# Routed expert rows: weighted at evacuation and summed by an accumulating scatter, in place of slots combined at the end

## The reference

```python
def moe(x, p):
    scores = sigmoid(x @ p['w_router'])                        # 1032 x 64
    _, e_idx = top_k(scores + p['router_bias'], 6)
    w = take_along_axis(scores, e_idx, axis=1)
    w = w / sum(w, axis=-1, keepdims=True) * ROUTED_SCALE
    ...
    routed = segment_sum(y_rows * row_w[:, None], row_tok)     # y_rows: swiglu of each expert on its rows
    shared = swiglu(x, p['w_sh_gate'], p['w_sh_up'], p['w_sh_down'])
    return routed + shared
x = layer_norm(DN_ALPHA * x + moe(x, p), p['ln2_g'], p['ln2_b'])
```

## Time and profile before

| what | us |
|---|---|
| median of three runs | 2399.06 (2397.37 to 2402.83) |
| the profiled execution, its own time | 2404.58 |
| its span, first to last instruction | 2402.6 |
| PE busy over the span | 2310.7 (96%) |
| DVE, ACT, POOL busy over the span | 871.5, 595.5, 341.9 |

### The profile page before, as it was taken

The page is one execution under the profiler, slowest core; times in us unless marked ns, Lnnn a source line. Parts: engine busy times, 40 slices in busy tenths (PEclk is TensorE's granted clock), DMA queues, the critical chain, the costliest instruction groups (busy, mean ns, idle before and its releaser), DMA issues.

```text
span 2402.6 us, 28164 instructions
## 1 busy us (share of the span) xinstructions
PE 2310.7 (96%) x9838; PEld 1349.4 (56%) x9838; DVE 871.5 (36%) x1733; ACT 595.5 (25%) x1288; POOL 341.9 (14%) x763
## 2 busy tenths in 40 slices
PE   8998999999999999999999999899999999999976
PEld 6455656667666666666664556445455454454422
DVE  0217888643366661001003558311111111111139
ACT  2126666554234430000001220011111111111111
POOL 0003444202000000000000000132232222222300
PEclk9998999999999999999999999999999999999978
DMA  6211000436411103111103130399999999998856
GB/s 210 99 64 34 2 2 2 163 118 246 122 31 35 31 22 111 40 40 35 40 9 111 70 123 18 104 342 353 341 350 344 346 344 347 345 345 333 322 226 267
DMA packets 127114, 389.57 MB, mean 162 GB/s; under 512 B 20660, under 2 KB 77964, under 8 KB 98336
## 3 DMA queue, kind: packets, MB, share of 16 engines
q1 hardware_dynamic: 105360, 304.02, 34.4%
q0 software_dynamic: 21664, 84.31, 9.6%
HBM read 362.02 MB, written 50.04 MB: 172 GB/s over the span
## 4 chain that ended last, share of the span: by engine, by line
PE 89%; DVE 6%; issue 2%; DMA 2%; ACT 1%; SPq 0%; ACTq 0%; DVEq 0%
PE PS L1081 26%; PE PS L1303 19%; PE PS L1314 9%; PE PS L669 8%; PE PS L782 5%; PE PS L1216 4%; PE PS L815 3%; PE PS L852 3%; PE PS L1200 2%; PE PS L952 2%; PE PS L1255 1%; PE PS L717 1%; PE PS L1352 1%; DVE arena L2264 1%; PE PS L1137 1%
## 5 line engine op out<-in xcount | busy, mean ns | idle before, releaser
L1081 PE MATMUL PS<-arena 128*128 128x344 f32 x2112 | 614.6, 453 | 3.1 <-ACT arena L1634 3.1
L1081 PEld LDWEIGHTS PS<-arena 128*128 128x128 f32 x2112 | 401.8, 190 | 214.0 <-issue 5.2
L1303 PE MATMUL PS<-arena 128*128 128x512 f32 x1056 | 464.1, 592 | 0.0
L1363 ACT ACTIVATE arena<-PS 128x512 f32<-128x512 f32 (+13 forms) x561 | 265.9, 502 | 663.0 <-PE PS L669 422.6
L669 PEld LDWEIGHTS PS<-arena 128*128 128x128 f32 (+3 forms) x1960 | 239.4, 160 | 190.8 <-issue 129.8
L669 PE MATMUL PS<-arena 128*128 128x128 f32 (+3 forms) x1960 | 292.4, 281 | 33.0 <-DVE arena L1867 8.1
L1303 PEld LDWEIGHTS PS<-arena 128*128 128x128 f32 x1056 | 195.9, 190 | 221.0 <-issue 221.0
L1314 PE MATMUL PS<-arena 128*128 128x512 f32 x528 | 242.9, 592 | 0.0
L2233 DVE TENSOR_TENSOR arena<-PS,arena 128x256 f32<-128x256 f32 x66 | 28.0, 425 | 437.7 <-ACT arena L1685 437.7
L1314 PEld LDWEIGHTS PS<-arena 128*128 128x128 f32 x528 | 95.5, 191 | 94.7 <-issue 94.7
L2298 POOL TENSOR_SCALAR arena<-arena 128x384 f32<-128x384 f32 (+3 forms) x192 | 103.2, 559 | 141.3 <-DVE arena L1844 95.8
(11 more groups left out here) (310 smaller groups left out, 2039.9 us busy)
## 6 DMA issues: line engine op xcount, KB each, us to landing
arena<-in_w_exp_gate SPq DMA_DIRECT2D x66, 1024.0 KB, 6.7
arena<-in_w_exp_up SPq DMA_DIRECT2D x66, 1024.0 KB, 8.8
arena<-in_w_exp_down SPq DMA_DIRECT2D x66, 1024.0 KB, 8.7
arena<-expert_rows SPq DMA_DIRECT2D x8, 3072.0 KB, 13.2
arena<-in_w_in SPq DMA_DIRECT2D x34, 512.0 KB, 3.8
...
```

What stands on the lines that cost most here:

```text
L1081: ins = mm(PS[:, bank + c, 0:CH], w[:, k, :], rhs[:, k, c * CH:(c + 1) * CH], start=k == 0, stop=k == kts - 1)
L1303: ins = mm(PS[:, 2 + s, :].rearrange("p (h n) -> p h n", h=2), xgT[:, s, k, :], wex[:, :, s, k, :], start=k == 0, stop=k == KT - 1)
L1363: return fn(out, in_, ACT.Copy)
```

## The change

Each token now has one row in DRAM, `acc_rows` (1032 rows of 4 KB in the memory of `expert_rows`). SP writes `x1tok` there (residual and shared expert) before the loop, and the six routed rows of a token are added to it by the scatters, whose DMA has an addition as compute operation. Because a token can be in several blocks, two scatters must not overlap: POOL waits for the landing of scatter 0 (`yd0`) before scatter 1, and for that of scatter 1 (`yd1`) before the scatter 0 of the next turn.

The weight of a routed row is multiplied in as its output is copied from PSUM: ACT's copy has a scale, DVE's copy becomes a product with a scalar per partition. The 128 weights of a block come by a small indirect gather of 4-byte elements (`weights_in`) from a table that SP writes to DRAM (`wtab`).

The loop is 32 fixed turns (64 blocks). Spare blocks follow one at a time (`spare`, all four engines, SP alike with `spare_in`), in three ranges (`SPARE`) with a branch around each. `nblk` now holds the number of blocks and the counts for which SP waits.

The tail reads the 4 MB of `acc_rows` back into `x1tok` in five transfers. For each tile DVE takes the statistics, ACT the root, DVE the reciprocal and the negative mean times it, ACT scales and shifts the whole tile, DVE multiplies by `ln2_g`, POOL adds `ln2_b`, and SP writes it out from `x1tok`. PE has no part in it.

A few semaphores are renamed and used twice (`s_load`), which changes no wait. The loop bodies of 32 turns and the branch ladder, the same on each engine, are shown for POOL alone:

```diff
+SPARE = ((NE // 2, NE // 2 + 2), (NE // 2 + 2, NE // 2 + 8), (NE // 2 + 8, NBLK // 2))
...
-        ygs = [at(o_, TOPK, D) for o_ in (4000, 30784, 36928, 45120)]
-        fin = at(10144, 2, D)
-        dg = at(21472, 2, 4, P)
+        ACC0 = 16
+        y_rows = y_dram.rearrange("b p d -> (b p) d")[0:ACC0 + NTOK, :]
+        acc_rows = y_rows[ACC0:, :]
+        wtab = y_dram.rearrange("b p d -> (b p d) ()")[0:NTOK * 8, :]
...
+        widx = rowb[:, 0, 0:2]
+        wrow = at(29700, 2)
...
+        Y_IN = {m: (s_load[k], 48 if k == 3 else 32) for k, m in enumerate((0, 1, 2, 4, 6))}
...
+            sp.wait_ge(sem("M_done"), NT)
+            sp.dma_start(wtab[0:SEQ * 8, :].rearrange("(t p k) o -> p t (k o)", p=P, k=8), wfin[:, 0:NT - 1, :]).then_inc(sem("wt_out"), 16)
...
-            turns = sp.value_load(nblk[0:1, 0:1], min_val=33, max_val=NBLK // 2)
-            with sp.Fori(1, NBLK // 2) as i:
-                with sp.If(i < turns):
...
+                sp.wait_ge(sem("acc_done"), t + 1)
+                sp.dma_start(acc_rows[t * P:t * P + n, :], x1tok[0:n, t, :]).then_inc(sem("x2_out"), 16)
+            blocks = sp.value_load(nblk[0:1, 0:1], min_val=NE, max_val=NBLK)
+            landed = [sp.value_load(nblk[0:1, 1 + s:2 + s], min_val=8 * NE, max_val=8 * NBLK) for s in range(2)]
...
+            for s in range(2):
+                sp.wait_ge(sem(f"yd{s}"), landed[s])
+            sp.wait_ge(sem("x2_out"), 16 * NT)
+            sp.dma_start(x1tok[0:BD, NT - 1, :], acc_rows[SEQ:NTOK, :]).then_inc(Y_IN[0][0], 16)
+            for (m, (s, _)), hi in zip(list(Y_IN.items())[1:], list(Y_IN)[2:] + [NT]):
+                sp.dma_start(x1tok[:, m - 1:hi - 1, :], acc_rows[(m - 1) * P:(hi - 1) * P, :].rearrange("(t p) d -> p t d", p=P)).then_inc(s, 16)
             for m, t in enumerate(TAIL):
                 n = rows_of(t)
...
                 sp.wait_ge(sem("fin_done"), m + 1)
                 dst = o["y_p"][t * P:(t + 1) * P, :] if n == P else o["y_s"]
-                sp.dma_start(dst, fin[0:n, m % 2, :]).then_inc(sem(f"y_out{m % 2}"), 16)
...
+                sp.dma_start(dst, x1tok[0:n, t, :]).then_inc(sem("y_out"), 16)
+            sp.wait_ge(sem("y_out"), 16 * NT)
...
-            with pe.Fori(0, NBLK // 2) as i:
-                with pe.If(i < turns):
...
-            for m, t in enumerate(TAIL):
-                n = rows_of(t)
-                pe.wait_ge(sem(f"y_in{m % 4}"), 16 * (m // 4 + 1))
...
+            with pe.Fori(0, NE // 2) as i:
...
+            def spare(i, s):
+                for hf in range(2):
+                    pe.wait_ge(sem(f"xgT_ev{hf}"), 2 * i + 2 + s)
+                pe.wait_ge(sem(f"wex{s}"), 32 * i + 32)
+                pe.wait_ge(sem(f"gu_free{s}"), i + 1)
+                gate_up(s, 0, KT).then_inc(sem(f"gu_mm{s}"), 1)
+                turn_hidden(i, s)
+                pe.wait_ge(sem("hT_ev"), 2 * i + s + 1)
+                pe.wait_ge(sem(f"wexd{s}"), 16 * i + 16)
+                pe.wait_ge(sem("y_ev"), 2 * i + s + 1)
+                pe.wait_ge(sem("y_ev2"), 2 * i + s + 1)
+                down(s, 0)
+                down(s, 1).then_inc(sem("y_mm"), 1)
+                turn_rows(i + 1, s, False)
...
+            def act_down(i, s, first=False):
+                act.wait_ge(sem("y_mm"), 2 * i + s + 3)
+                if not first:
+                    act.wait_ge(sem(f"yd{s}"), 16 * i)
+                act.wait_ge(sem(f"wg{s}"), 16 * i + 16)
+                fn(ysb[:, s, 512:1024], PS[:, 5 + 2 * s, :], ACT.Copy, scale=wrow[:, s:s + 1]).then_inc(sem("y_ev"), 1)
...
-            def weights_diag(m):
...
+                s, y = st[0:n, m % 2, :], x1tok[0:n, t, :]
                 act.wait_ge(sem("var_done"), NT + m + 1)
-                fn(st[0:n, m % 2, 14:15], st[0:n, m % 2, 13:14], ACT.Sqrt).then_inc(sem("std_done"), 1)
-                if m + 2 < NT:
-                    weights_diag(m + 2)
+                E.do(fn(s[:, 14:15], s[:, 13:14], ACT.Sqrt), sem("std_done"))
+                act.wait_ge(sem("mean_done"), m + 1)
+                E.do(fn(y, y, ACT.Identity, bias=s[:, 0:1], scale=s[:, 15:16]), sem("normed"))
...
-            E.step(ts(wk[0:1, 3:4], cs[0:1, NE - 1:NE], 0.5, None, ALU.mult))
-            E.step(ts(ridx[0:1, 1:NE + 0], const("exp", 1)[:, 0:NE - 1], wk[0:1, 3:4], None, ALU.is_lt))
...
-            E.step(V.tensor_copy(nblk[0:1, 0:1], wk[0:1, 4:5]), sem("table_step"))
+            E.step(ts(wk[0:1, 3:4], cs[0:1, NE - 1:NE], float(NE), None, ALU.add))
+            E.step(ts(wk[0:1, 4:5], wk[0:1, 3:4], 1.0, None, ALU.add))
+            E.step(V.tensor_copy(nblk[0:1, 0:1], wk[0:1, 3:4]))
+            E.step(V.tensor_copy(nblk[0:1, 3:4], wk[0:1, 4:5]))
+            E.step(ts(nblk[0:1, 1:2], nblk[0:1, 3:4], 1, None, ALU.logical_shift_right))
+            E.step(ts(nblk[0:1, 2:3], nblk[0:1, 0:1], 1, None, ALU.logical_shift_right))
+            E.step(ts(nblk[0:1, 1:3], nblk[0:1, 1:3], 4, None, ALU.logical_shift_left), sem("table_step"))
...
+            def dve_down(i, s, first=False):
+                dve.wait_ge(sem("y_mm"), 2 * i + s + 3)
+                if not first:
+                    dve.wait_ge(sem(f"yd{s}"), 16 * i)
+                dve.wait_ge(sem(f"wg{s}"), 16 * i + 16)
+                ts(ysb[:, s, 0:512], PS[:, 4 + 2 * s, :], wrow[:, s:s + 1], None, ALU.mult).then_inc(sem("y_ev2"), 1)
...
-            def normed_out(m):
...
-                E.step(stt(y, y, s[:, 12:13], lnw[0:n, 2, :], ALU.subtract, ALU.mult))
...
-                E.do(stt(fin[0:n, m % 2, :], y, s[:, 15:16], lnw[0:n, 3, :], ALU.mult, ALU.add), sem("fin_done"))
+            with dve.Fori(1, NE // 2) as i:
...
+            def scaled_out(m):
+                n = rows_of(TAIL[m])
+                y = x1tok[0:n, TAIL[m], :]
+                dve.wait_ge(sem("normed"), m + 1)
+                E.do(tt(y, y, lnw[0:n, 2, :], ALU.mult), sem("scaled"))
             for m, t in enumerate(TAIL):
                 n = rows_of(t)
-                acc = x1tok[0:n, t, :]
                 s = st[0:n, m % 2, :]
-                dve.wait_ge(sem(f"y_in{m % 4}"), 16 * (m // 4 + 1))
-                for k in range(VK):
-                    E.step(stt(acc, ygs[m % 4][0:n, k, :], wfin[0:n, t, k:k + 1], acc, ALU.mult, ALU.add), sem("yg_used") if k == VK - 1 else None)
-                dve.wait_ge(sem("comb_mm"), m + 1)
-                acc2 = acc.rearrange("p (a b) -> p a b", a=2)
-                E.step(tt(acc2, acc2, PS[0:n, 4 + 2 * (m % 2):6 + 2 * (m % 2), :], ALU.add), sem("acc2_done"))
-                stats(acc, s)
+                if m in Y_IN:
+                    dve.wait_ge(*Y_IN[m])
+                stats(x1tok[0:n, t, :], s)
                 if m:
-                    normed_out(m - 1)
+                    scaled_out(m - 1)
                 dve.wait_ge(sem("std_done"), NT + m + 1)
                 E.step(V.reciprocal(s[:, 15:16], s[:, 14:15]))
-            normed_out(NT - 1)
+                E.do(stt(s[:, 0:1], s[:, 12:13], -1.0, s[:, 15:16], ALU.mult, ALU.mult), sem("mean_done"))
+            scaled_out(NT - 1)
...
+            def weights_in(s):
+                G.indirect_dma_start(out=wrow[:, s:s + 1], out_offset=None, in_=wtab,
+                                     in_offset=bass.IndirectOffsetOnAxis(ap=widx[:, s:s + 1], axis=0),
+                                     bounds_check=NTOK * 8 - 1, oob_is_err=False).then_inc(sem(f"wg{s}"), 16)
+            def rows_out(i, s, first=False):
                 pool.wait_ge(sem("y_ev"), i * 2 + s + 3)
                 pool.wait_ge(sem("y_ev2"), i * 2 + s + 3)
+                if s:
+                    pool.wait_ge(sem("yd0"), 16 * i + 16)
+                elif not first:
+                    pool.wait_ge(sem("yd1"), 16 * i)
                 G.tensor_tensor(pause[:, 0:1], izero[:, 0:1], izero[:, 0:1], ALU.add)
-                G.tensor_tensor(dsts[:, s:s + 1], slotall[:, bass.ds(i * 2 + s, 1)], izero[:, 0:1], ALU.add).then_inc(sem(f"ix{s}"), 1)
-                pool.wait_ge(sem(f"ix{s}"), n)
+                G.tensor_tensor(dsts[:, s:s + 1], tokall[:, bass.ds(i * 2 + s, 1)], izero[:, 1:2], ALU.add).then_inc(sem(f"ix{s}"), 1)
+                G.tensor_tensor(widx[:, s:s + 1], slotall[:, bass.ds(i * 2 + s + 2, 1)], izero[:, 0:1], ALU.add).then_inc(sem(f"ix{s}"), 1)
+                pool.wait_ge(sem(f"ix{s}"), i * 3 + 5)
                 G.tensor_tensor(pause[:, 1:2], izero[:, 0:1], izero[:, 0:1], ALU.add)
-                G.indirect_dma_start(out=yrows, out_offset=bass.IndirectOffsetOnAxis(ap=dsts[:, s:s + 1], axis=0),
+                G.indirect_dma_start(out=y_rows, out_offset=bass.IndirectOffsetOnAxis(ap=dsts[:, s:s + 1], axis=0),
                                      in_=ysb[:, s, :], in_offset=None,
-                                     bounds_check=NTOK * 8 - 1, oob_is_err=False).then_inc(sem(f"yd{s}"), 16)
+                                     bounds_check=ACC0 + NTOK - 1, oob_is_err=False, compute_op=ALU.add).then_inc(sem(f"yd{s}"), 16)
```

(36 more changed lines are left out.)

235 lines of the change are left out of this document (119 added, 116 removed).

## The result

| | before | after |
|---|---|---|
| median, us | 2400.34 (2397.37 to 2402.83, 4 runs) | 2447.53 (2443.44 to 2454.28, 4 runs) |
| ratio, 95% interval | | 1.0199 (1.0174 to 1.0225) |
| span of the profiled execution, us | 2402.6 | 2452.5 |
| granted clock over the span | 0.980 | 0.966 |

The account below looks back on a forecast made before the run. PE was taken to bound the loop's turns and DVE to pace the tail. The terms, -8.6 - 62.9 + 1 + 28 = -42.5 us from 2399.06, gave 2356.6, stated as 2358; 8 in 10 range 2328 to 2420.

Parts of the forecast that it names:

- Part 1: Expert loop: 64 blocks in 32 turns and the 65th alone in 13.5 us instead of 22.15; gain 8.6 us.
- Part 2: From last expert matmul to the end: 44.6 us instead of 107.46, DVE tiles of 3.4 us; gain 62.9 us.
- Rival C: Tail: engines don't overlap, DVE and ACT wait for each other; 5 us a tile, 2371 us; no chance of its own.
- Part 3: Ahead of the loop: two more small DVE steps, a memset, SP's writes of tables and rows; together 1 us of loss.
- Part 4: Loop: waits for adding scatters make a 24.2 us chain to the row gather, over 22.83; 0.9 us a turn, 28 us.
- the spread: Loop: landings range from 5.2 to 9.7 us and only late ones count; 0.2 us more a turn.
- D: Loop: extra landing time of an adding scatter over a plain one; taken as 1.5 us, bounds 0 and 5.1.
- A: Loop: adding scatter lands like a plain one, the 22.2 us chain fits into 22.83; 2337 us, chance 0.21.
- B: Loop: POOL's pair of scatter waits becomes the period; slower than before, over 2400, up to 2493 us; chance 0.16.

Follow-up runs that it names:

- e4_tail_ts: Changed kernel with the tail's one-column product as a tensor_scalar reading one tensor instead of a scalar_tensor_tensor reading two; 2436.37 us, ratio 1.0158 to the kernel before.
- e1_plain: Changed kernel with the addition taken out of the scatter's DMA, all waits and other transfers kept; 2364.71 us, ratio 0.9854 to the kernel before.
- e2_noweights: Changed kernel without the gathers of weights in the loop, all weights 1; 2425.59 us, ratio 1.0103 to the kernel before.
- e3_gathers_first: Changed kernel with the row gathers issued between scatter 0 and scatter 1, one turn further ahead; 2351.07 us, ratio 0.9795 to the kernel before.
- e8_first_plain: e3_gathers_first with scatters that only store and don't add; 2352.15 us, ratio 0.9791 to the kernel before.
- e9_first_delay: e3_gathers_first with seven more small POOL steps ahead of each scatter; 2352.79 us, ratio 0.9820 to the kernel before.

## Why the prediction was wrong

**Part 1, the turns: right.** 65 blocks were run (65 scatters in the list above), the lone one in 13.0 us; 13.5 were forecast.

**Part 2, the tail: 44.6 forecast, 64.4 measured.** The order of the steps was as described. Mis-sized was the tile: of the "two small steps (0.17 each)" one took 2.33 us with its wait for POOL, which makes a tile 1.9 us longer, 15 us in all. L2272 of the earlier trace rows was rightly read, but before there was no POOL addition beside such a step. e4_tail_ts shows this for the step. The rest is smaller: the first 7.4 us took 9.0, since the last scatter landed in 4.69 us rather than 3.2, and the end after the last DVE product took 7.9 instead of 5.1: POOL's addition of 2.34 and 5.5 us more to the end, for which the earlier trace rows had 3.0. Rival C named the right size (5 us a tile) and the wrong reason: not ACT's place in the order but POOL's. It would have been 13 us on the bill.

**Part 3: 1 us of loss forecast, 1.9 us gained.** The loop starts that much earlier. No run asks why.

**Part 4, the loop: 28 us forecast, 104 measured, and this is what turned the sign.** The mechanism stood in the text: a chain from the first down product over two scatters and a row gather, a slack that falls to nearly nothing, a late gather that holds PE and is paid by half in each turn. What failed is the sizes of its terms, of the row gather behind the adding scatter above all, and that PE's clock behind a stall was left out. Worked out over the 16 stalls of after (the first row from the turn shown above):

| step of the chain | forecast, us | measured, us |
|---|---|---|
| down product to issue of scatter 0 | 2.25 | 2.5 |
| scatter 0 to scatter 1 | 7.6 + 1.5 + 1.37 = 10.5 | 11.95 |
| scatter 1 to the row gather | 1.03 + 1.6 + 1.15 = 3.8 | 4.1 |
| row gather to PE's restart | 7.2 + 0.5 = 7.7 | 9.0 |
| sum | 24.2 | 27.5 |
| over 22.83 | 1.4 | 4.7 |
| PE's slower clock behind a stall | none | 1.9 |
| a turn, half of the two | 0.7, and 0.2 for the spread | 3.3 |

The chain was 3.3 us too short, and as it stood only 1.4 us over the period, an error of a seventh made the excess three times as large.

The table hides two misreadings that cancel. The 7.6 and 7.2 us of the earlier trace rows mix both scatters and both row gathers; scatter 0 alone took 8.7 us before and the first row gather alone 6.2, which adds 1.1 and takes off 1.0, so the chain with plain landings is 22.2 either way. Against these bases the steps are:

- D, the landing of scatter 0: +1.9 us (10.6 for 8.7, and e1_plain has 8.7 with every wait in place). D = 1.5 was near.
- The row gather: +2.7 us (8.9 for 6.2 over the 16 stalls), where +0.5 stood for a weights gather ahead of it. This is the term that failed most. In e1_plain the same gather lands in 6.5 us, so most of it goes with the addition of the scatter ahead, and e2_noweights shows that next to nothing goes with the weights.
- The issue of scatter 1 on POOL: 1.60 us where the 1.03 of the earlier trace rows was kept.
- PE's clock behind a stall: not counted. It is some 30 of the 104 us (16 x 1.9).

The adding scatter is the source of the first three. The rule of the Trainium skill that the prediction named (page Collectives: The Full Stack, section "The bandwidth ceiling: the fold count and why AG ≠ RS ≠ AR": a second source read halves the rate) is borne out for the engines' time: half of the queue's traffic doubled would be 17.4 x 1.5 = 26%, measured were 27.4%. By that rule D was some 1.1 us and the landing of scatter 0 grew by 1.9; on the gather that is queued behind, where most of the price lay, it says nothing. Nor do the profiles show the rise to 379 GB/s that the prediction worked out: the rate is 350 with the addition and 351 without (e3_gathers_first and e8_first_plain, 1900 to 2000 us); whether its count of bytes takes in the reads of the destination is not shown.

**The rivals.** A (2337) falls: D isn't near 0, and even with plain scatters the chain doesn't quite fit (e1_plain, 23.16 us a turn), where A had 22.2 of 22.83. B had the right side, with another mechanism: it made POOL's pair of waits the period. In after POOL doesn't always wait for a landing (24 of 45 pauses over 1650 to 2250 us; 45 is the number of scatters there), and PE waits for gathers. In e3_gathers_first POOL does wait for the landing at 52 of 53 pauses, and the pair stands at PE's very period (9.7 and 10.4 from issue to landing, and twice 1.35), yet the turn is 22.8, and e9_first_delay shows that it yields when it is stretched. B's break-even of D = 3.6 was thus for the wrong loop: the chain with the row gather broke even much earlier. The tail, the lone block and the earlier start gave 54 us. By the table the loop uses them up at 1.7 us a turn, which is 3.4 us per pair of turns with 1.9 of clock in it: a chain of 24.3. The forecast's own 24.2 stood there already, had the clock been counted and the tail been priced at its measured 43 us.

**The range.** It ended at 2420 because D above 2.2 was given a chance of only 0.24, and the other terms of the chain no spread at all. With the measured D of 1.9 and nothing else changed the text's own chain gives 24.6, 0.9 + 0.2 us a turn, 2362 us; by this chain not even its upper bound of 5.1 (2412 us) leaves the range. The terms that did carry it out had been given no spread.
